# State-space scan: both directions' outputs within a tile by one product per head, no state behind the last tile, edge sums as five products

## What is computed

```python
# per direction; x (t, 16 heads, 64), dt (t, 16), da = dt * A, b and c (t, 2 groups, 128)
ac     = cumsum(da)                                   # within a chunk
decay  = exp(where(tril, ac[l] - ac[s], -inf))
y_diag = einsum(c[l] . b[s] * decay[l, s], x[s] * dt[s])
states = einsum(b[s], x[s] * dt[s] * exp(ac[-1] - ac[s]))
s      = exp(ac[-1]) * s + states                     # from chunk to chunk
y_off  = c[l] . s * exp(ac[l])
y      = y_diag + y_off                               # forward + flipped backward, + d * x, * silu(z)
```

## Time and profile before

| what | value |
|---|---|
| median of the three runs | 2118.55 us |
| lowest and highest of them | 2113.12 and 2122.88 us |
| the profiled execution, its own time | 2117.31 us |
| its span (first to last recorded instruction) | 2115.5 us |
| TensorE / VectorE / ScalarE / GpSimd busy | 2031.9 / 723.9 / 572.6 / 89.1 us |
| DMA | 193.53 MB, mean 91 GB/s |
| mean granted TensorE clock | 0.987 |

### The profile page before, as it was taken

How to read it: one execution, slowest core, us unless ns; L and a number is a source line. 1 busy time by engine, 2 the same in 40 slices (tenths; PEclk the granted TensorE clock), 3 DMA queues, 4 the chain that set the end, 5 groups by cost and what they waited for, 6 DMA issues and landing times.

```text
span 2115.5 us, 29493 instructions
## 1 busy us (share of the span) xinstructions
PE 2031.9 (96%) x12484; PEld 1251.5 (59%) x12484; DVE 723.9 (34%) x1441; ACT 572.6 (27%) x1224; POOL 89.1 (4%) x86
## 2 busy tenths in 40 slices
PE   6999999999998999999999999998989997999997
PEld 2444777776664444444444465444766665888886
DVE  2541676104672010000000046456767855010001
ACT  4121113514462020000000032224355788110000
POOL 0000231000000000000000000000211110000000
PEclk9999999999999999999999999999989999999999
DMA  6433010233301212211221122112224210234442
GB/s 271 159 144 139 23 38 23 77 123 120 121 2 40 90 60 80 80 69 70 80 75 70 59 100 100 60 60 80 82 75 170 79 54 9 101 138 151 147 149 90
DMA packets 28001, 193.53 MB, mean 91 GB/s; under 512 B 3004, under 2 KB 4285, under 8 KB 5854
## 3 DMA queue, kind: packets, MB, share of 16 engines
q1 hardware_dynamic: 27826, 191.51, 24.7%
q10 hardware_dynamic: 44, 0.14, 0.0%
HBM read 190.59 MB, written 1.05 MB: 91 GB/s over the span
## 4 chain that ended last, share of the span: by engine, by line
PE 88%; DVE 6%; ACT 4%; issue 1%; DMA 1%; POOL 0%; SPq 0%; ACTq 0%; DVEq 0%; POOLq 0%
PE psum L706 87%; ACT ws_sb L1497 1%; DVE ws_sb L1968 1%; DVE gl_tmp_sb L1968 1%; ACT arena_sb L1497 1%; DVE hT_sb L1971 1%; DVE arena_sb L1968 1%; DMA arena_sb<-w 1%; DVE ws_sb L1971 0%; ACT wide_sb L1497 0%; DVE arena_sb L1977 0%; PE psum L1112 0%; ACT L1497 0%; PE psum L965 0%; ACT const_sb L1497 0%
## 5 line engine op out<-in xcount | busy, mean ns | idle before, releaser
L706 PE MATMUL psum<-hT_sb,ring_sb 128*128 128x512 f32 (+2 forms) x2272 | 797.9, 512 | 1.9 <-ACT hT_sb L1497 1.9
L706 PEld LDWEIGHTS psum<-hT_sb,ring_sb 128*128 128x128 f32 (+1 forms) x2272 | 428.4, 189 | 363.6 <-issue 339.2
L706 PE MATMUL psum<-arena_sb,ring_sb 128*128 128x512 f32 (+1 forms) x1216 | 396.3, 487 | 5.0 <-DVE small_sb L1974 1.9
L1497 ACT ACTIVATE ws_sb<-psum 128x512 f32<-128x512 f32 (+3 forms) x256 | 141.2, 552 | 770.4 <-PE psum L706 740.1
L706 PEld LDWEIGHTS psum<-arena_sb,ring_sb 128*128 128x128 f32 x1216 | 231.8, 191 | 166.8 <-issue 143.9
L706 PE MATMUL psum<-ring_sb,hT_sb 128*128 128x256 f32 (+3 forms) x1248 | 244.6, 374 | 0.5 <-ACT hT_sb L1497 0.5
L706 PEld LDWEIGHTS psum<-ring_sb,hT_sb 128*128 128x128 f32 (+1 forms) x1248 | 195.7, 177 | 59.1 <-issue 28.3
L1968 DVE TENSOR_TENSOR arena_sb<-ws_sb,psum 128x512 f32<-128x512 f32 (+1 forms) x44 | 24.4, 554 | 414.6 <-PE psum L706 414.6
L1971 DVE SCALAR_TENSOR_TENSOR xT_sb<-psum,mod_sb,xT_sb 128x256 f32<-128x256 f32 x48 | 23.2, 483 | 386.8 <-PE psum L706 386.3
L1497 ACT ACTIVATE wide_sb<-xT_sb 128x512 f32<-128x512 f32 (+1 forms) x40 | 21.8, 544 | 392.2 <-PE psum L706 295.1
L1971 DVE SCALAR_TENSOR_TENSOR ws_sb<-ws_sb,cols_sb 128x512 f32<-128x512 f32 (+1 forms) x176 | 123.8, 703 | 6.3
(11 more groups left out here) (167 smaller groups left out, 1474.0 us busy)
## 6 DMA issues: line engine op xcount, KB each, us to landing
ring_sb<-w SPq DMA_DIRECT2D x146, 1024.0 KB, 4.8
hT_sb<-w SPq DMA_DIRECT2D x16, 1024.0 KB, 4.8
arena_sb<-w SPq DMA_DIRECT2D x8, 1024.0 KB, 17.4
ring_sb<-w SPq DMA_DIRECT2D x8, 768.0 KB, 4.1
xT_sb<-x SPq DMA_DIRECT2D x1, 2048.0 KB, 8.6
const_sb<-consts SPq DMA_DIRECT2D x1, 2048.0 KB, 9.4
y<-xT_sb SPq DMA_DIRECT2D x1, 1024.0 KB, 4.8
ring_sb<-w SPq DMA_DIRECT2D x2, 256.0 KB, 3.8
```

The lines of the kernel that those rows point to most:

```text
L706: return nc.tensor.matmul(o, l, r, start=start, stop=stop)
L1497: return nc.scalar.activation(o, i, func, **kw)
```

## The change

- Units become 16 passes w of a tile, a group and half a group. `decay(w)` is two products, one for each direction, accumulated in the same bank. Since one direction's sums are zero where the other's are not, a single exponential gives both decays.
- The two directions' `dt` go into the scores: ScalarE writes backward mask times backward `dt` into the new buffer `g_dt` (four 128x128 copies with a scale per partition), VectorE adds forward mask times forward `dt` (four 128x128 scalar-tensor-tensor operations), and `p_seg` is `e_seg` times `g_dt`. The head products use `x0` itself; `xdt` is gone. A pass has four head products for both directions.
- `dt` goes into the edge factors by one small operation, and `xw` is made from `x0` by one operation for each of six tiles (three for each direction).
- The last tile of each direction (k = 3) makes no state: no product into bank 0, no scaling and adding of `st0`. The head products are added to `y0` in `add_diag`, eight times in all.
- The pairs now follow each pass, w = 0 to 15, in the old order of directions and tiles, while the passes go through tiles 0 to 3 once.
- The edge sums are five products: four of 64 columns, one of 128. The eight b.c products go to banks 0 and 1, and stand behind the wait for the last query tiles; the wait for `late_taken` moves behind the first two z0 parts.
- GpSimd's 32 products alternate between the directions, with one buffer for each.

```diff
             def edges(layer):
...
-                for j in range(TT):
+                for kind, sums in enumerate((beyond, upto_incl)):
                     for d in DIRS:
-                        mm(psum[:, 4, j * 96 + d * 16:j * 96 + d * 16 + 16], beyond[d], da[:, j, d * 16:d * 16 + 16])
-                        mm(psum[:, 4, j * 96 + 32 + d * 16:j * 96 + 48 + d * 16], upto_incl[d], da[:, j, d * 16:d * 16 + 16])
-                    last = mm(psum[:, 4, j * 96 + 64:j * 96 + 96], ones, da[:, j, :])
+                        at = 128 * kind + 64 * d
+                        mm(psum[:, 4, at:at + 64], sums[d], da[:, :, d * 16:d * 16 + 16])
+                last = mm(psum[:, 4, 256:384], ones, da.rearrange("p j (d h) -> p d j h", d=2))
...
             def ssd():
                 late_columns(4)
                 edges(0)
-                pe.wait_ge(S["late_taken"], 5)
-                for g in range(SSD_G):
-                    for j in range(TT):
-                        last = mm(psum[:, 5 + g, j * P:(j + 1) * P], bT[:, g, j * P:(j + 1) * P], cT[:, g, j * P:(j + 1) * P])
-                last.then_inc(S["ssd_bc"], 1)
                 for g in (2, 3):
                     for i in range(2):
                         drained(pe, out_of("qk0", g, i))
+                for g in range(SSD_G):
+                    for j in range(TT):
+                        last = mm(psum[:, g, j * P:(j + 1) * P], bT[:, g, j * P:(j + 1) * P], cT[:, g, j * P:(j + 1) * P])
+                last.then_inc(S["ssd_bc"], 1)
                 z0_part(0)
                 z0_part(1)
+                pe.wait_ge(S["edge"], 1)
+                pe.wait_ge(S["late_taken"], 5)
                 pe.wait_ge(S["ssd_masked"], 4)
-                pe.wait_ge(S["edge"], 1)
...
+                def decay(w):
+                    if w > 1:
+                        pe.wait_ge(S["ssd_exp"], w - 1)
+                    for d in DIRS:
+                        u = 2 * w + d
+                        pe.wait_ge(S["ssd_r"], u + 1)
+                        mm(psum[:, 4 + w % 2, :], beyond[d], g_decay[:, d].rearrange("p a b -> p (a b)"),
+                           start=(d == 0), stop=(d == 1)).then_inc(S["ssd_seg"], 1)
 
                 decay(0)
...
+                for w in range(16):
+                    if w + 1 < 16:
+                        decay(w + 1)
+                    for n in (2 * w + 2, 2 * w + 3):
+                        if n < 32:
+                            z0_part(n)
+                        else:
+                            first_values(n - 32)
+                    jd, gd, hq = w // 4, w // 2 % 2, w % 2
+                    pe.wait_ge(S["ssd_p"], w + 1)
+                    if hq == 0 and w >= 4:
+                        pe.wait_ge(S["ssd_summed"], w // 2 - 1)
                     for i in range(4):
                         h = hq * 4 + i
-                        last = mm(psum[:, 6 + v % 2, h * 64:(h + 1) * 64], p_seg[:, u % 2, i], xdt[m % 2][:, g * 8 + h])
+                        at = (gd * 8 + h) * SSD_P
+                        last = mm(psum[:, 6 + w // 2 % 2, h * 64:(h + 1) * 64], p_seg[:, w % 2, i], x0[:, jd, at:at + SSD_P])
                     last.then_inc(S["ssd_diag"], 1)
...
+                    d, k, g = w // 8, w // 2 % 4, w % 2
+                    j, m = TILE_AT[d][k], 3 * d + k
+                    if w > 0:
+                        pe.wait_ge(S["ssd_y"], w)
+                    if k > 0:
+                        last = mm(psum[:, 1, :], cT[:, g, j * P:(j + 1) * P], st0[:, g])
+                    if k < 3:
+                        pe.wait_ge(S["ssd_x"], m + 1)
                         last = mm(psum[:, 0, :], b_tok[:, j, g * P:(g + 1) * P],
                                   xw[m % 2][:, g * 8:(g + 1) * 8].rearrange("p a b -> p (a b)"))
-                        last.then_inc(S["ssd_pair"], 1)
+                    last.then_inc(S["ssd_pair"], 1)
...
+                act.wait_ge(S["ssd_masked"], 4)
+                for w in range(16):
+                    j, g, h0 = w // 4, w // 2 % 2, w % 4 * 4
+                    if w > 1:
+                        act.wait_ge(S["ssd_p"], w - 1)
+                    for i in range(4):
+                        h = h0 + i
+                        ins = f(g_dt[:, w % 2, i], g_mask[:, 1, g, j], ACT.Copy, scale=dt[:, j, 16 + h:17 + h])
+                    own(ins.then_inc(S["ssd_dt"], 1), S["ssd_dt"])
+                    act.wait_ge(S["ssd_seg"], 2 * w + 2)
+                    own(f(e_seg[:, w % 2], psum[:, 4 + w % 2, :].rearrange("p (a b) -> p a b", a=4), ACT.Exp).then_inc(S["ssd_exp"], 1), S["ssd_exp"])
+                    if w % 2 == 1:
+                        z_copy(w // 2)
...
+                link(tt(edge[:, :, 0:32], edge[:, :, 0:32], dt, ALU.mult))
...
-                    link(tt(xdt[m % 2], xj, bc(dt[:, j, d * 16:d * 16 + 16], 2, SSD_P), ALU.mult))
-                    own(tt(xw[m % 2], xdt[m % 2], bc(edge[:, j, d * 16:d * 16 + 16], 2, SSD_P), ALU.mult).then_inc(S["ssd_x"], 1), S["ssd_x"])
+                    own(tt(xw[m % 2], per_head(x0[:, j]), bc(edge[:, j, d * 16:d * 16 + 16], 2, SSD_P), ALU.mult).then_inc(S["ssd_x"], 1), S["ssd_x"])
+
+                def scores(w):
+
+                    j, g, h0 = w // 4, w // 2 % 2, w % 4 * 4
+                    dve.wait_ge(S["ssd_dt"], w + 1)
+                    for i in range(4):
+                        ins = stt(g_dt[:, w % 2, i], g_mask[:, 0, g, j], dt[:, j, h0 + i:h0 + i + 1], g_dt[:, w % 2, i], ALU.mult, ALU.add)
+                    link(ins)
+                    dve.wait_ge(S["ssd_exp"], w + 1)
+                    if w > 1:
+                        dve.wait_ge(S["ssd_diag"], w - 1)
+                    own(tt(p_seg[:, w % 2], e_seg[:, w % 2], g_dt[:, w % 2], ALU.mult).then_inc(S["ssd_p"], 1), S["ssd_p"])
+
+                def add_diag(q):
+
+                    j, g = q // 2, q % 2
+                    y = y0[:, j, g * 512:(g + 1) * 512]
+                    dve.wait_ge(S["ssd_diag"], 2 * q + 2)
+                    own(tt(y, y, psum[:, 6 + q % 2, :], ALU.add).then_inc(S["ssd_summed"], 1), S["ssd_summed"])
...
                 inputs(0)
...
+                for w in range(16):
+                    scores(w)
+                    if w > 0:
+                        accumulate(w - 1)
+                    if w % 2 == 0:
+                        m = w // 2 + 1
+                        if m < 8 and m % 4 < 3:
+                            inputs(m - m // 4)
+                        if w > 0:
+                            add_diag(w // 2 - 1)
+                add_diag(7)
                 accumulate(15)
...
             for u in range(32):
...
+                w, d = u // 2, u % 2
+                at = d * 16 + w % 4 * 4
+                if u > 1:
                     pool.wait_ge(S["ssd_seg"], u - 1)
...
+                own(tt(g_decay[:, d], bc(da[:, w // 4, at:at + 4], 2, P), bc(upto_incl[d], 1, 4)).then_inc(S["ssd_r"], 1), S["ssd_r"])
```

More of the change, by code:

```diff
@@ L400, in backbone @@
         p_seg = area(ws, 4096, 2, 4, P)
-        xdt = [area(w, at, SSD_H, SSD_P) for w, at in ((ws, 5120), (extra, 0))]
+        g_dt = area(ws, 5120, 2, 4, P)
         xw = [area(w, at, SSD_H, SSD_P) for w, at in ((ws, 6144), (extra, 1024))]
@@ L594, in backbone @@
             l2_sq l2_sum merged mix_rs mix_transposed mixed banks_zeroed mod_columns mod_copied mod_rows mod_taken mod1_used rows_copied rows_spread rs scaled
-            square square_used ssd_bc ssd_diag ssd_exp ssd_masked ssd_p ssd_pair ssd_r ssd_seg ssd_x ssd_y
+            square square_used ssd_bc ssd_diag ssd_dt ssd_exp ssd_masked ssd_p ssd_pair ssd_r ssd_seg ssd_summed ssd_x ssd_y
             dt_copied dt_turned late_rows late_copied late_columns late_taken summed neg_eg beta_lanes inv_zeroed z_done z_taken z_ready
@@ L1068, in decay @@
[L1068 to L1072, removed]
-                decay(0)
[L1075 to L1089, removed]
+                def decay(w):
[6 more added lines that the diff above has]
+                           start=(d == 0), stop=(d == 1)).then_inc(S["ssd_seg"], 1)
@@ L1452, in _ @@
             pe.wait_ge(S["gl_ready"], 1)
-            pe.wait_ge(S["ssd_exp"], 32)
+            pe.wait_ge(S["ssd_exp"], 16)
             pe.wait_ge(S["z_taken"], 8)
@@ L1599, in edges @@
                 act.wait_ge(S["edge_sums"], layer + 1)
-                own(f(edge[:, :, :], psum[:, 4, 0:TT * 96].rearrange("p (a b) -> p a b", a=TT), ACT.Exp).then_inc(S["edge"], 1), S["edge"])
+                own(f(edge.rearrange("p a (k b) -> p a k b", k=6), psum[:, 4, 0:TT * 96].rearrange("p (k a b) -> p a k b", k=6, a=TT),
+                      ACT.Exp).then_inc(S["edge"], 1), S["edge"])
             def z_copy(fill):
@@ L2090, in ssd, with per_head @@
                     for d in DIRS:
-                        own(tt(g_mask[:, d, g], psum[:, 5 + g, :].rearrange("p (a b) -> p a b", a=TT), bc(upto_incl[d], 1, TT), ALU.mult).then_inc(S["ssd_masked"], 1), S["ssd_masked"])
```

(25 more changed lines are left out.)

9 lines of the change are left out of this document (removed).

## The result

The changed kernel takes 2094.84 us (median of four runs, 2094.08 to 2095.40), the kernel before 2115.84 (four runs, 2112.43 to 2122.88). The ratio is 0.989, with a 95% interval of 0.9871 to 0.9908: 1.1% faster, 21 us, inside the stated range and 1.4 us above the stated time.

A forecast was written before the change was run, and what follows sets the result against it. TensorE was taken to bound the kernel, the other engines waiting for it. Savings 8.5 + 17.7 - 1.3 + 0.2 = 25.1 us gave 2092.2 against the profiled 2117.31, or 2093.4 as median; range 2086 to 2099, up to 2104 with rivals.

The forecast's parts named there:

- Ahead of the loop: Edge sums, b-c products and two z0 parts fall from 14.72 to 6.2 us at full clock: 8.5 saved.
- The loop: Shorter passes save 14.2 us and the last tile's missing state products 3.4: together 17.7 of 138.89 us.
- a stall: Once, at the loop's start: the second decay waits for two fresh GpSimd products, taken as 1.3 us (0.4 to 2.5).
- The pass: One loop pass on TensorE takes 7.79 us instead of 8.68, saving 0.89 sixteen times.
- the state products: In the loop, no state behind the last tile: four products of 128x512 fewer, 0.86 us each, 3.4 saved.
- Behind the loop: VectorE's shorter tail lets the product with z0 start earlier; between 0 and 0.45 us gained, taken as 0.2.
- VectorE hidden: In the loop, VectorE's work falls from 92 to about 75 of 123 us and stays hidden behind TensorE.
- ScalarE hidden: In the loop, ScalarE gains 64 scaled copies, 20 us on 29, all hidden behind TensorE.
- Rival A: In the loop, two GpSimd operations per pass block VectorE, making it the bound: 2095 us (mild, 12%) or 2116 (hard, 4%).

The follow-up runs named there:

- kernels 1 and 2: The second of the two: the changed kernel with the twenty edge products of before put back; 2100.85 us, ratio 0.9916 (0.9899 to 0.9933).
- kernel 1: The kernel before with only the edge sums changed, to five products; 2112.11 us against 2118.01 for the kernel before, ratio 0.997.
- kernel 4: The changed kernel with the last tile's four state products put back on TensorE; 2097.56 us, loop 125.52 us.
- kernel 6: The changed kernel with two GpSimd decay buffers for each direction instead of one; 2093.32 us, in a second measurement 2094.05 beside 2093.88 for the changed kernel.
- kernel 7: The changed kernel with dummy 128x128 VectorE operations added per pass: four more took 2093.30 us, twelve more 2125.36 us.

## Why the prediction was right

It forecast 25.1 us. The profiled execution's own time fell by 21.9, from 2117.31 to 2095.37, the medians by 21.0, and by 24.9 in the later measurement beside 9 executions of the kernel before. By its terms:

- **Ahead of the loop,** 8.5 forecast, 14.72 - 6.44 = 8.28 measured; an edge instruction took 0.12, not 0.105. The mechanism holds (kernels 1 and 2). But the term was read from one profile, in which the clock was low for 10.2 us. Against the second profile of the same kernel it is 11.42 - 6.44 = 5.0. That is the weak step: the time of the low clock before was taken for a constant, and it varies between runs. The 8.28 comes so close because it is counted against the very profile that the term was read from. The variation fits the kernel before spreading over 2112 to 2123 us, and kernel 1 gaining 5.9. That five products keep the clock up is shown (kernels 1 and 2); whether it is their number, their columns or the length of the run that does it is not separated.
- **The loop,** 17.7 less a stall of 1.3 is 16.4 forecast, 16.8 measured. The pass is 7.78 for 7.79; the state products are 3.43 for 3.4 (kernel 4); the stall is 0.93 for 1.3 (kernel 6).
- **Behind the loop,** 0.2 forecast. From `gates(0)` to `gates(1)` it is 9.23 us instead of 9.53, a gain of 0.3.
- **VectorE hidden.** Its work in the loop was mis-sized, 75 us for 86. The step at fault took 0.31 and 0.69 for operations undisturbed by GpSimd, though the earlier trace rows showed the score product disturbed; the new 128x128 operations came out 6 us and the scalings of the state 5 us dearer. Its cover was real nevertheless: kernel 7 adds another 17 us for nothing.
- **ScalarE hidden.** 20 us of copies on 29 were forecast, 49; it was busy for 39.6. The step left out that sixteen of the thirty-two exponentials go, at 0.60 us each. It changed nothing, because ScalarE had room either way.

These make 25.4 us in the stretch from the edge sums to `gates(1)`. Of that 3.5 do not reach the end of this execution. TensorE comes to the edge sums 0.84 us later, because its first weights landed later; the change does not touch that. Most of the rest shows behind the stage, in the gated delta rule (the first line is of the kernel before, in the second fence the changed one):

```profile
1488.00:1830.00 342.00, 312.92 (x4686) 225.50 (x4682) 213.88 (x521) 211.51 (x553) 39.18 (x43) 0.96 0.22 79
```

```profile
1463.80:1808.00 344.20, 316.23 (x4677) 226.75 (x4677) 213.73 (x520) 211.31 (x553) 39.05 (x43) 0.95 0.22 79
```

Nearly the same work takes 2.2 us more at a slightly lower mean clock. The other profiles speak against the change as its cause: the program behind the loop is the same in all of them, and from the loop's end to the end of the span it takes 1753.5 us in the first profile of the kernel before and 1755.8 in that of the changed one, but 1751.8 in the second of the kernel before, 1755.5 in kernel 1 (the old loop), and 1753.0 to 1758.5 in the others (the new loop). The 2.3 us lie within that spread. What makes it vary was not tested.

Rival A's two whole blocks in each pass, 2.1 us at the least, were not paid. What VectorE's groups show over undisturbed operations is some 13 us over the loop (an estimate: 6 for the 128x128 operations, 5 for the scalings, 2 for the rest), 0.8 a pass. By the Trainium skill's rule of the exclusive port lock (SBUF — State Buffer, "SBUF: two separate sides") an operation that comes second waits for the whole of the other. The trace agrees in kind: scaling the state took 1.41 in passes where GpSimd ran and 0.69 in the last.

## What to carry to other kernels

Where an engine is busy throughout a stage and the others demonstrably wait for it, price an edit by that engine's steps from start to start, instruction by instruction: such a sum came out within 0.4 us over 139. Small float32 products, up to 128 columns here, are paid by their number, not by their columns, so gather them; and read a low granted clock in one profile as one draw, to be taken again before it is counted as a gain. Before putting work on a waiting engine, measure its slack by adding dummy work: four operations for each pass were free, twelve cost everything the change had won.

## What the runs showed that was not expected

- The clock's fall behind eight 2-column and some 17 to 40 of the 16-column instructions, with TensorE busy all the time, came in all four profiles of kernels with twenty edge products, for 3.4, 3.4, 6.8 and 10.2 us. It came in none of the nine with five.
- Beside GpSimd's products, small VectorE operations suffer too: 64 of 128x128 took 0.41 us each in the mean instead of 0.31 (6 us together), and eight scalings of the state 1.32 instead of 0.69 (5 us).
- With gaps of 0.2 to 2.75 us on TensorE, in a loop that is otherwise dense, the clock came down in four places (0.94 on the average). It added some 8.5 us to the 20.1 us of gaps; the loop was 31.7 us longer.
